# Level products of a triangular inverse in 32x32 tiles, TensorE's list reordered, and eight products a head whose result nobody reads

## The reference

```python
a_mat = eye + jnp.where(pos[:, None] > pos[None, :], beta[..., :, None] * decay * kk, 0.0)
rhs = jnp.concatenate([beta[..., None] * v, (beta * gamma)[..., None] * k], axis=-1)
sol = lax.linalg.triangular_solve(a_mat, rhs, left_side=True, lower=True, unit_diagonal=True)
v_t, w = sol[..., :dv], sol[..., dv:]
p_qk = jnp.einsum('bhnck,bhnmk->bhncm', q, k) * decay
def step(h, xc):
    qg_c, pqk_c, vt_c, w_c, kd_c, gl_c = xc
    u = vt_c - jnp.einsum('bhck,bhkv->bhcv', w_c, h)
    o = jnp.einsum('bhck,bhkv->bhcv', qg_c, h) + jnp.einsum('bhcm,bhmv->bhcv', pqk_c, u)
    h = h * gl_c[..., None, None] + jnp.einsum('bhck,bhcv->bhkv', kd_c, u)
    return h, o
```

## Time and profile before

| | before |
|---|---|
| median of 3 runs | 3042.48 us (3040.59 to 3049.66) |
| profiled execution | 3039.26 us, span 3037.5 us |
| TensorE matmul busy | 2944.0 us, 97% |
| VectorE busy | 1787.7 us, 59% |
| ScalarE busy | 968.5 us, 32% |
| mean granted clock of TensorE | 0.991 |
| mixer's heads | about 1922 to 2174 us |

### The profile page before, as it was taken

One profiled execution on the slowest core, in us unless ns is written; L12 is line 12 of the kernel. 1 busy time (PEld: TensorE's weight loads), 2 busy tenths in 40 slices (PEclk: granted clock), 3 DMA queues, 4 the chain that ended last, 5 costly groups with the idle time before them and its releaser, 6 DMA issues. The chain is left out here.

```text
span 3037.5 us, 43085 instructions
## 1 busy us (share of the span) xinstructions
PE 2944.0 (97%) x17705; PEld 2438.0 (80%) x17705; DVE 1787.7 (59%) x2027; ACT 968.5 (32%) x1203; POOL 24.4 (1%) x35
## 2 busy tenths in 40 slices
PE   6899999999999999999979999999999999999998
PEld 3588888888888888888868899777777888888887
DVE  3337555565656566565674576666556655666666
ACT  3222222222222122222263256322345343444333
POOL 0000000000000000000000000000000000000000
PEclk9999999999999999999989999999999999999999
DMA  9725454443644556575823344100254555555553
GB/s 370 271 97 198 138 177 153 152 158 134 208 138 166 208 208 235 180 289 181 307 82 100 111 141 139 51 12 9 95 183 164 184 192 193 180 193 180 194 193 125
DMA packets 307695, 508.01 MB, mean 167 GB/s; under 512 B 8252, under 2 KB 230020, under 8 KB 291684
## 3 DMA queue, kind: packets, MB, share of 16 engines
q1 hardware_dynamic: 305312, 496.79, 48.4%
q0 software_dynamic: 1408, 8.83, 0.7%
q10 hardware_dynamic: 836, 0.33, 0.0%
HBM read 503.78 MB, written 2.15 MB: 167 GB/s over the span
## 5 line engine op out<-in xcount | busy, mean ns | idle before, releaser
L2264 PE MATMUL ps<-xn,parts 128*128 128x512 f32 (+1 forms) x8992 | 1782.0, 360 | 7.0 <-DVE parts L1531 3.2
L2264 PEld LDWEIGHTS ps<-xn,parts 128*128 128x128 f32 x8992 | 1516.9, 189 | 270.9 <-issue 6.4
L880 ACT ACTIVATE parts<-raw 128x1024 fp32r<-128x1024 f32 x634 | 656.3, 1055 | 1085.8 <-PE ps L2264 876.3
L1531 DVE TENSOR_TENSOR parts<-raw,parts 128x1024 fp32r<-128x1024 f32 x632 | 755.5, 1220 | 406.5 <-ACT parts L880 406.1
L2264 PE MATMUL ps<-parts,h_parts 128*128 128x512 f32 x3168 | 729.2, 390 | 1.6 <-DVE h_f L1576 1.5
L2264 PEld LDWEIGHTS ps<-parts,h_parts 128*128 128x128 f32 x3168 | 591.6, 188 | 134.4 <-issue 6.1
L1564 DVE SCALAR_TENSOR_TENSOR macc<-raw,cs,macc 128x2048 f32<-128x2048 f32 x150 | 348.0, 2345 | 0.0
L1666 DVE TENSOR_TENSOR acc<-acc,ps 128x512 f32<-128x512 f32 x160 | 110.0, 687 | 212.5 <-PE ps L2264 212.5
L918 ACT ACTIVATE h_parts<-h_f 128x512 fp32r<-128x512 f32 (+1 forms) x42 | 35.1, 837 | 355.6 <-DVE h_f L1623 355.6
L1623 DVE TENSOR_TENSOR h_f<-silu_g,ps 128x1024 f32<-128x1024 f32 x20 | 24.4, 1221 | 147.2 <-PE ps L2264 147.2
L2264 PE MATMUL ps<-parts,xn 128*128 128x512 f32 x384 | 91.6, 394 | 0.0
(11 more groups left out here) (247 smaller groups left out, 1233.7 us busy)
## 6 DMA issues: line engine op xcount, KB each, us to landing
raw<-in_w_mod SPq DMA_DIRECT2D x132, 1024.0 KB, 6.0
raw<-in_w_up SPq DMA_DIRECT2D x88, 1024.0 KB, 5.1
raw<-in_w_down SPq DMA_DIRECT2D x88, 1024.0 KB, 5.3
raw<-in_w_gate SPq DMA_DIRECT2D x84, 1024.0 KB, 5.1
raw<-in_w_in SPq DMA_DIRECT2D x41, 1024.0 KB, 5.3
raw<-in_w_out SPq DMA_DIRECT2D x16, 1024.0 KB, 5.1
extra<-in_w_mod SPq DMA_DIRECT2D x12, 1024.0 KB, 14.3
gate_raw<-in_w_gate SPq DMA_DIRECT2D x4, 1024.0 KB, 14.2
```

Source lines behind the costliest of these rows:

```text
L880: nc.scalar.activation(parts[:, unit % PART_SLOTS, 0, :], raw[:, slot, b * UNIT:(b + 1) * UNIT], ACT.Copy).then_inc(hi_ready, 1)
L1531: nc.vector.tensor_tensor(parts[:, pslot, 1, :], raw[:, slot, b * UNIT:(b + 1) * UNIT], parts[:, pslot, 0, :].bitcast(F32), ALU.subtract)\
L2264: return nc.tensor.matmul(o, lhsT, rhs, start=start, stop=stop)
```

## The change

The level products now work on the 32x32 blocks alone: four products a chunk, one on each row group of 32 partitions, each writing its own 32 partitions of the bank; y takes its operand from n_T directly. The masked product is 256 columns wide in place of 512 and has a tile of its own, `c_Y`; the masks are stored half as wide. After each of the eight level products of a head stands `keep_awake`, a product of the identity with itself into the last 128 columns of a bank, which nobody reads. In TensorE's list `decay_sums` and `products_k` of head i + 2 move from the start of the next iteration into the end of iteration i, around `solve_v`. The end products of `token_k(m, 0)` and of the second value tiles come before the transposes. The tile `pT` is filled in another arrangement (four VectorE instructions for three), so that the scan's last two output products take one matmul each.

```diff
-N_PAIR = 8
+N_PAIR = 6
...
-    masks += [pair(level(s)) for s in (2, 4, 8, 16)]
+    masks += [np.concatenate([own(level(s)) for s in (2, 4, 8, 16)], 1)]
...
-        g_Y = ra("g_Y", [P, STEPS, CHUNK])
+        c_Y = ra("c_Y", [P, STEPS, BLOCK])
...
-                a.ago(2, "y_mm", "s_init")
+                a.ago(2, "s_init")
...
             def level_Y(m, lv):
                 m.wait("y_mm", lv + 1)
-                nc.vector.tensor_tensor(g_Y[:], ps[:, B_Y, :].rearrange("p (s c) -> p s c", c=CHUNK), every(LEVEL[lv]),
-                                        ALU.mult).then_inc(hs["y_ok"], 1)
+                nc.vector.tensor_tensor(c_Y[:], blocks(B_Y), every(LEVEL[lv]), ALU.mult).then_inc(hs["y_ok"], 1)
...
-                S = c_S[:, m.h % 2]
-                X = ps[:, B_X, :].rearrange("p (s c) -> p s c", c=CHUNK)[:, :, 0:BLOCK]
-                nc.vector.tensor_tensor(S, S, X, ALU.subtract).then_inc(hs["s_ok"], 1)
+                S = flat(c_S[:, m.h % 2])
+                nc.vector.tensor_tensor(S, S, ps[:, B_X, 0:STEPS * BLOCK], ALU.subtract).then_inc(hs["s_ok"], 1)
...
-                for rows, t, of in ((low, slice(0, 4), slice(0, 4)), (high, slice(0, 3), slice(2, None, -1)),
-                                    (high, slice(3, 4), slice(3, 4))):
-                    nc.vector.tensor_tensor(pT[rows, m.h % 2, t, rows], p_h[rows, of, :], incl_b[rows, of, :],
+                for rows, t, cols, of in ((low, slice(0, 2), low, slice(0, 2)), (low, slice(2, 4), high, slice(2, 4)),
+                                          (high, slice(0, 2), high, slice(2, 0, -1)), (high, slice(2, 4), low, slice(0, 4, 3))):
+                    nc.vector.tensor_tensor(pT[rows, m.h % 2, t, cols], p_h[rows, of, :], incl_b[rows, of, :],
...
             def token_k(m, g, a):
+                k_bank_free(m, g, a)
+                if g == 0:
+                    token_ends(B_A, m.h, g)
+                    inc(token_tiles(B_A, m.h, g), "kT")
+                else:
+                    token_tiles(B_B, m.h, g)
+                    inc(token_ends(B_B, m.h, g), "kT")
...
-                    m.wait("nd_ok")
+                    m.wait("n_ok")
                 for s in range(STEPS):
-                    last = pair_mm(B_Y, CHUNK * s, n_D[:, m.h % 2, s, :], twice(c_T, m, s))
+                    for q, rows in enumerate((Q0, Q1, Q2, Q3)):
+                        last = mm(ps[rows, B_Y, BLOCK * s:BLOCK * s + BLOCK], n_T[rows, m.h % 2, s, SIDES[q % 2]],
+                                  c_T[rows, m.h % 2, s, :])
...
                 for s in range(STEPS):
-                    last = pair_mm(B_X, CHUNK * s, g_Y[:, s, :], twice(c_S, m, s))
+                    for rows in (Q0, Q1, Q2, Q3):
+                        last = mm(ps[rows, B_X, BLOCK * s:BLOCK * s + BLOCK], c_Y[rows, s, :], c_S[rows, m.h % 2, s, :])
...
+            def keep_awake(bank):
+
+                mm(ps[:, bank, 384:512], ident, ident)
...
-                    if t < 2:
-                        last = mm(o[:, t:4 - t:3 - 2 * t, :], u, pT[:, b.h % 2, t, :], False, False)
-                    else:
-                        mm(o[:, t, :], u, pT[:, b.h % 2, t, 0:CHUNK], False, False)
-                        last = mm(o[:, 3 - t, :], u, pT[:, b.h % 2, t, CHUNK:P], False, t == 3)
+                    c0 = min(t, 3 - t)
+                    last = mm(o[:, c0:4 - c0:3 - 2 * c0, :], u, pT[:, b.h % 2, t, :], False, t == 3)
...
-                if a:
+                if a and i <= 0:
                     decay_sums(a)
                     products_k(a)
...
                 y_level(m, 0)
+                keep_awake(B_X)
...
                 x_level(m, 0)
+                keep_awake(B_Y)
...
                 if i == HEADS - 1:
                     token_v(m, 1)
+                else:
+                    v_bank_free(m, 1)
+                    token_ends(B_A, HEADS + m.h, 1)
                 if b:
                     scan_read(b, 6)
...
-                    token_v(m, 1)
+                    inc(token_tiles(B_A, HEADS + m.h, 1), "vT")
...
                 solve_w(m)
                 if b:
                     out_sums(b)
+                then = Head(pe, i + 2) if i + 2 < HEADS else None
+                if then:
+                    decay_sums(then)
                 solve_v(m, 0)
                 solve_v(m, 1)
+                if then:
+                    products_k(then)
```

More of the change, by code:

```diff
@@ L285, in build_layer @@
         Q0, Q1, Q2, Q3 = (slice(BLOCK * q, BLOCK * q + BLOCK) for q in range(4))
-        LEVEL = [c2[:, n * CHUNK:(n + 1) * CHUNK] for n in range(LEVELS)]
-        y_off = g_Y[:].rearrange("p s c -> p (s c)")[:, 0:STEPS * BLOCK].rearrange("p (s c) -> p s c", c=BLOCK)
+        LEVEL = [c2[:, n * BLOCK:(n + 1) * BLOCK] for n in range(LEVELS)]
         cv = sb("cv", [P, 4, TOK], R_QZ + 8192)
@@ L460, in build_layer @@
             "kT": 2, "kd_ok": 2, "kbg_ok": 2, "vT": 2, "vb_ok": 2, "qg_ok": 1,
-            "qk_mm": 1, "p_half": 1, "p_ok": 3, "f_a": 1, "f_mid_ok": 1, "f_b": 1, "f_even": 1, "f_v": 2, "f_hi": 1,
+            "qk_mm": 1, "p_half": 1, "p_ok": 4, "f_a": 1, "f_mid_ok": 1, "f_b": 1, "f_even": 1, "f_v": 2, "f_hi": 1,
             "f_lo": 1,
@@ L727, in outer_Y @@
                 m.wait("y_mm")
-                nc.scalar.activation(y_off, blocks(B_Y), ACT.Copy).then_inc(hs["y_ok"], 1)
+                nc.scalar.activation(c_Y[:], blocks(B_Y), ACT.Copy).then_inc(hs["y_ok"], 1)
             def outer_forward(m):
@@ L1984, in token_tiles, with token_ends @@
                     t0 = 256 * g + CHUNK * n
-                    nc.tensor.transpose(ps[:, bank, P * n:P * n + P], kv[:, tile, t0:t0 + P], ident)
+                    last = nc.tensor.transpose(ps[:, bank, P * n:P * n + P], kv[:, tile, t0:t0 + P], ident)
+                return last
+            def token_ends(bank, tile, g):
                 for rows, c_ in zip(HALVES, (4 * g + 3, 4 * g)):
@@ L1988, in token_tiles, with k_bank_free @@
                 return last
-            def token_k(m, g, a):
+            def k_bank_free(m, g, a):
                 if g == 0:
@@ L1998, in token_k, with v_bank_free @@
                     m.last("p_half")
-                inc(token_tiles((B_A, B_B)[g], m.h, g), "kT")
-            def token_v(m, g):
+            def token_k(m, g, a):
+                k_bank_free(m, g, a)
[5 more added lines that the diff above has]
+                    inc(token_ends(B_B, m.h, g), "kT")
+            def v_bank_free(m, g):
                 if g == 0:
@@ L2005, in token_v @@
                     m.wait("vb_ok", 1)
-                inc(token_tiles(B_A, HEADS + m.h, g), "vT")
+            def token_v(m, g):
+                v_bank_free(m, g)
+                token_tiles(B_A, HEADS + m.h, g)
+                inc(token_ends(B_A, HEADS + m.h, g), "vT")
             def products_q(m):
@@ L2030, in fnet_positions @@
                 inc(last, "f_b")
-            def twice(blocks_of, m, s):
-                return blocks_of[:, m.h % 2, s, :].unsqueeze(1).to_broadcast([P, 2, BLOCK])
             def y_level(m, lv):
@@ L2072, in outer_x @@
                     cols = slice(BLOCK * s, BLOCK * s + BLOCK)
-                    mm(ps[Q0, B_X, cols], y_off[Q1, s, :], c_S[Q1, m.h % 2, s, :])
-                    last = mm(ps[Q3, B_X, cols], y_off[Q2, s, :], c_S[Q2, m.h % 2, s, :])
+                    mm(ps[Q0, B_X, cols], c_Y[Q1, s, :], c_S[Q1, m.h % 2, s, :])
+                    last = mm(ps[Q3, B_X, cols], c_Y[Q2, s, :], c_S[Q2, m.h % 2, s, :])
                 inc(last, "x_mm")
```

## The result

| | before | changed |
|---|---|---|
| median of runs | 3045.48 us (3040.59 to 3049.66, 4 runs) | 3080.9 us (3072.05 to 3090.14, 4 runs) |
| profiled execution, span | 3039.26 us, 3037.5 us | 3074.31 us, 3072.5 us |
| mixer, head 0 to the end of head 7 | 250.65 us | 285.05 us |
| mean granted clock | 0.991 | 0.977 |

The changed kernel takes 1.0122 times as long, interval 1.0092 to 1.0153. It is slower by 1.2%, where 0.25% less was forecast, and it lies outside the range. All but 0.6 us of the 35.0 us between the two spans is in the mixer, which is taken here from the first level product of head 0 to the end of the last value product of head 7.

A forecast was written before the change was run, and what follows sets the result against it. TensorE, busy 97%, bounds the kernel by its list. Seven middle heads -5.6 us, head 0 -1.6 (0.1 given back), last scan -0.4: total -7.5, so 3031.8, plus 3.2 to the median: 3035.0 us; range 3026 to 3051.

The forecast's parts named there:

- Four row groups run together: Eight level products a head: next step 0.63 us after each instead of 1.08, gain 3.6 us a head.
- rival 1: Level products: four row groups do not run at once, 1.13 us each, kernel at 3067 us; chance 12%.
- Unread products: Eight keep_awake products a head: 0.44 us each, cost 3.5 us a head, 2.0 in head 0.
- The order and pT: TensorE's list: fewer shape changes save about 0.3 us a head, the scan's merged pT products another 0.3.
- Waits for VectorE and ScalarE: TensorE's two u_buf waits a head, 0.6 us together, stay or shrink a little: -0.1 us.
- rival 3: VectorE and ScalarE chain takes over, TensorE waits at x_level(0), u_buf or c_T: 3039 to 3045 us; chance 15%.
- Nothing hides them, for the list has no idle time there: Unread products in TensorE's list: their full time counts, 3.5 us a head, 2.0 in head 0.
- the pricing from start to start: TensorE's list: each product priced by the distance between starts of neighbouring rows, which holds the drain as well.
- a waits term: Middle head: TensorE's waits for u_buf change by -0.1 us, bounds -0.5 and +0.3.
- Rival 2: Mixer heads: clock falls to 1.2 GHz despite unread products; one 6.6 us low stretch a head gives 3057 us; chance 8%.

The follow-up runs named there:

- the list alone: Changed kernel with level products back in 64x64 tiles and no unread products; new order and merged pT products stay: 3035.89 us, ratio 0.9976.
- half of the small products: Reordered list with merged pT products, nothing unread, only the x level products in 32x32 tiles, y in 64x64: 3030.86 us, ratio 0.9948 to the kernel before.
- the thinnest kernel: Changed kernel with its eight keep_awake calls a head removed, all level products still in 32x32 tiles: 3048.83 us.

## Why the prediction was wrong

- **Four row groups run together: right.** The level product costs 0.68 us for the 0.63 taken; rival 1 (1.13) is out. Neither rule of the Trainium skill that spoke against it holds for this product. "TensorEngine Tiling (Array Packing)", Restrictions and Gotchas, forbids row tiles one PSUM bank; here four write one bank, each its own 32 partitions of it, 64 records in 0.75 us (tiles that write the same partitions no run tries). "TensorE: Matmul & The Clock Gate", section "Wait — 56ns, not 53.3ns?", has a floor of about 25 ns from start to start; the 64 records give about 11 ns each (0.68 / 64).
- **Unread products: right in price, wrong in purpose.** 0.42 us for 0.44. With them the clock was low for 82 us, without them for 75.
- **The order and pT: right.** With the waits 0.7 us a head over seven heads, 4.9 us, were forecast for the mixer; 5.0 were measured with the list alone.
- **Waits for VectorE and ScalarE: right.** The u_buf waits stayed (0.18 and 0.39), the mask product took 0.41 us; rival 3 did not come.
- **The failing step** is "Nothing hides them, for the list has no idle time there", and with it the pricing from start to start. It takes as given that the next instruction is always there. The sum had a waits term of -0.1 us a head, bounds -0.5 and +0.3, which held only waits for other engines; measured it is 6.7 us of stand-stills, about +0.8 a head and so nearly all of the forecast gain of 7.5. And the sum had no term at all for what such a wait does to the clock; by 81.9 low microseconds at 0.42 that is 34.4 us, and it alone takes the time out of the range. The number was at hand: rival 1 says that the list goes from 550 records in 31.3 us to some 800 in a head, and I read that as a question to the row groups, not to the fetch of instructions.
- **Rival 2, the clock, had 8% and is what decided,** but not by the mechanism given. I dismissed it because thin stretches stand at 1.00 in the earlier trace rows. Thin products did not need to be the cause: the falls came behind pauses, and a semaphore's pause of 1.39 us brings them with 64x64 products, four times in seven. My only row on a fall had 3.57 us of idle time, and I took it as if that were the least. The size was off too: 81.9 us low for eight times 6.6 (the stretch of the earlier trace rows itself is 6.8 us long in the clock's own record). "TensorE: Matmul & The Clock Gate" of the Trainium skill, section "HAM oscillation — how this bites in real kernels", has a kernel whose clock falls behind waits for transfers of 3 to 5 us; here falls follow gaps of 0.7 to 2.1 us, and the measurement decides.

What stays open: why one stand-still of 0.9 to 1.6 us has a fall behind it and another has none, why a low stretch lasts 10 us here and 30 us there, and why the clock fell in head 7 of five kernels behind 0.25 us. All seven falls of the changed kernel's two traces came 1.6 to 3.5 us after a stand-still began, so for them the account holds; that idle time is the only cause is not shown, and the load of the array in the neighbourhood, the rival, may have a part. That the block comes too late is inferred from place, packet size, density and the landings; no run changes the fetch itself, and what decides when a packet is sent was not looked into.

## What to carry to other kernels

Cutting products into smaller tiles multiplies instructions; before pricing the shorter list, work out how long its densest blocks of 256 instructions take (weight loads and the sequencer's instructions count too) and compare that with the shortest distance between two instruction packets that a trace shows, 3.2 us here. Where TensorE has no slack, a stand-still of one microsecond can cost ten times its length through the clock (30.7 low microseconds are 12.9 us), so take the part of a change that stays under that rate (here half of the small products, 0.5% faster) and leave the rest. Products put in to keep the clock up are worth one run without them.

## What the runs showed of the hardware

- Kernels whose densest 1024 TensorE instructions ran at 53 a microsecond or less had no stand-still for want of instructions, those at 57.5, 65, 72 and 78 had some. They come at one place in every 256 instructions, last 0.3 to 2.1 us, and all 54 end 1.2 to 1.5 us after a packet of 16 KB has landed. A packet takes 0.9 to 1.4 us in the changed kernel's mixer, and in no trace's mixer do two start less than 3.2 us apart.
- Four 32x32 tiles on four row groups, all into one PSUM bank (each its own partitions), run at once: 64 records in 0.75 us.
- TensorE's clock dropped to 1.2 of 2.4 GHz within 4 us of the start of an idle time of 0.7 to 2.1 us, in the thinnest kernel also behind two or three waits of 0.4 to 0.6 us, and stayed there for 3.4 to 37.5 us. Idle times as long passed without a drop (0.98, 1.00, 1.39 and 1.63 us), and at one place five kernels had a drop behind 0.25 us.
